# Sample attention of a two-layer decoder step: cached pages turned on VectorE in 32x32 blocks, scores formed in four row groups of TensorE

## The reference, cut to what matters

```
past = cache_latent[l][page_table].reshape(8, 2048, 288)
keys = concat([past, latent])                              # 2048 + 8 rows of 288
q_lat = einsum('bqhn,chn->bqhc', q_nope, w_uk)             # queries taken into the latent
s = einsum('bqhd,bkd->bhqk', concat([q_lat, q_rope]), keys) * SCALE, masked causally
p = softmax(s)
o = einsum('bhqk,bkd->bqhd', p, keys[..., :256])
```

## Time and profile before

| | |
|---|---|
| time, median of 3 runs | 2258.92 us (2255.19 to 2260.28) |
| time of the profiled execution | 2255.74 us |
| its span, first to last instruction | 2254.0 us |
| mean granted TensorE clock | 0.997 |
| busy: TensorE / VectorE / ScalarE / GpSimd | 2210.7 / 1170.6 / 874.9 / 655.1 us |
| transferred | 230.69 MB, mean 102 GB/s |
| chain that ended last | TensorE 96%, VectorE 2%, ScalarE 1% of the span |

### The profile page before, as it was taken

One profiled execution on the slowest core, in us unless ns is written; L12 is line 12 of the kernel. 1 busy time (PEld: TensorE's weight loads), 2 busy tenths in 40 slices (PEclk: granted clock), 3 DMA queues, 4 the chain that ended last, 5 costly groups with the idle time before them and its releaser, 6 DMA issues.

```text
span 2254.0 us, 42639 instructions
## 1 busy us (share of the span) xinstructions
PE 2210.7 (98%) x16239; PEld 1981.8 (88%) x16239; DVE 1170.6 (52%) x1831; ACT 874.9 (39%) x1815; POOL 655.1 (29%) x316
## 2 busy tenths in 40 slices
PE   7999999999999999999999999999999999999998
PEld 5899997667789999999988999966677999999998
DVE  4443753844346666651153717457443476666433
ACT  4223225832234555541132332366322355555322
POOL 0223433400022333333322334342000323333332
PEclk9999999999999999999999999999999999999999
DMA  9554332033333222235545333212332422222332
GB/s 302 170 145 100 85 85 66 19 109 108 85 130 91 79 84 84 84 109 167 173 126 176 83 97 83 79 43 63 97 108 57 156 70 83 79 80 83 87 85 84
DMA packets 338278, 230.69 MB, mean 102 GB/s; under 512 B 62732, under 2 KB 321605, under 8 KB 338140
## 3 DMA queue, kind: packets, MB, share of 16 engines
q1 hardware_dynamic: 336594, 226.37, 35.1%
q10 hardware_dynamic: 1546, 2.43, 0.4%
HBM read 223.15 MB, written 5.60 MB: 101 GB/s over the span
## 4 chain that ended last, share of the span: by engine, by line
PE 96%; DVE 2%; ACT 1%; DMA 0%; issue 0%; DVEq 0%; SPq 0%; ACTq 0%
PE PS L1550 62%; PE PS L1518 7%; PE PS L2000 5%; PE PS L2047 5%; PE PS L1912 3%; PE PS L1833 2%; PE PS L1646 2%; PE PS L1594 2%; PE PS L1936 2%; PE PS L1567 1%; PE PS L1889 1%; PE PS L1994 1%; PE PS L1950 1%; PE PS L2076 0%; DMA rows_in<-x_sample 0%
## 5 line engine op out<-in xcount | busy, mean ns | idle before, releaser
L975 POOL TENSOR_TENSOR wlo<-raw,whi 128x1024 fp32r<-128x1024 f32 (+1 forms) x248 | 586.0, 2363 | 1493.5 <-ACT whi L563 1493.5
L1550 PE MATMUL PS<-h_hi,whi 128*128 128x288 f32 x2496 | 740.7, 297 | 1.2 <-issue 1.0
L1550 PE MATMUL PS<-h_hi,wlo 128*128 128x288 f32 x2496 | 737.1, 295 | 0.0
L1550 PE MATMUL PS<-h_lo,whi 128*128 128x288 f32 x2496 | 737.0, 295 | 0.0
L563 ACT ACTIVATE whi<-raw 128x1024 fp32r<-128x1024 f32 (+1 forms) x252 | 258.4, 1025 | 919.6 <-PE PS L1550 823.5
L1550 PEld LDWEIGHTS PS<-h_hi,whi 128*128 128x128 f32 x2496 | 470.9, 189 | 9.4 <-issue 8.8
L1550 PEld LDWEIGHTS PS<-h_lo,whi 128*128 128x128 f32 x2496 | 471.0, 189 | 0.2
L1550 PEld LDWEIGHTS PS<-h_hi,wlo 128*128 128x128 f32 x2496 | 470.5, 188 | 0.0
L1452 DVE TENSOR_SCALAR conv<-zext,convp 128x592 f32<-128x592 f32 x88 | 153.6, 1746 | 132.5 <-ACTq L894 132.1
L1550 PE MATMUL PS<-act_hi,whi 128*128 128x288 f32 x704 | 209.9, 298 | 0.0
L1550 PE MATMUL PS<-act_hi,wlo 128*128 128x288 f32 x704 | 207.8, 295 | 0.0
(11 more groups left out here) (288 smaller groups left out, 3410.8 us busy)
## 6 DMA issues: line engine op xcount, KB each, us to landing
raw<-w_up SPq DMA_DIRECT2D x88, 512.0 KB, 3.8
pages<-cache_latent SPq DMA_DIRECT2D x256, 144.0 KB, 2.1
raw<-w_in SPq DMA_DIRECT2D x64, 512.0 KB, 4.0
ada_ring<-w_ada SPq DMA_DIRECT2D x41, 512.0 KB, 4.9
raw<-w_down SPq DMA_DIRECT2D x32, 512.0 KB, 3.9
ada_next<-w_ada SPq DMA_DIRECT2D x17, 512.0 KB, 4.0
ada_first<-w_ada SPq DMA_DIRECT2D x16, 512.0 KB, 10.4
raw<-w_out SPq DMA_DIRECT2D x16, 512.0 KB, 4.5
```

The lines of the kernel that those rows point to most:

```text
L975: nc.gpsimd.tensor_tensor(wlo[:, slot, 0:n], raw[:, slot, 0:n], whi[:, slot, 0:n].bitcast(F32), ALU.subtract).then_inc(lo_ready.sem, 1)
L1550: r = mm(PS[0:m, 2 * (j % pairs) + half, 0:HT], w, o[:, k0 + k, half * HT:half * HT + HT], start=(first and k == 0 and part is whi and o i ...
```

## The change

VectorE takes over the turning of the pages. One `transpose` (`turned_keys`) takes 32 columns of all 16 pages, 128 x 512 numbers in a step, and turns each 32x32 block in place of the array: in partition quarter r it leaves the 32 dimensions of the chunk for the 32 positions that quarter r held. Nine such chunks (the rotary one first) make one sequence; they go through a ring of four buffers. TensorE multiplies each chunk in four products with contraction 32, one for each partition quarter r, into bank r. Bank r so holds the positions of quarter r of every page, and the exponential writes `sc` back in page order by its access pattern. `turn_rope`, `turn_keys`, their copies and `rope_scores` are gone.

The queries must now lie in each quarter for every chunk (`qrep`, nine chunks less the rotary one): SP copies them by transfers for b = 0 and 1, ScalarE for the others in 16 small copies (`spread_queries`). The rotary queries are spread by three transfers instead of by VectorE. SP reads the 16 page numbers of a sequence before it waits for the buffer. VectorE takes one maximum over the four banks. ScalarE copies three groups of turned probabilities, VectorE two. On VectorE the first four chunks of b+1 are turned before the gate tile of b, and the others at the head of the next round. On TensorE all nine chunks of sequence 0 now stand ahead of the values of the last pair of heads.

```diff
     pages = [at(f"pages{i}", [128, NPG, LAT], o) for i, o in enumerate((raw_at, arena, cq_at + KD * B))]
-    keysT = [at("keysT0", [128, 2, 512], ckv_at), at("keysT1", [128, 2, 512], arena + 18432)]
-    ropeT = [at("ropeT0", [128, 512], ckv_at + 4096), at("ropeT1", [128, 512], arena + 22528)]
+    NT, RING = LAT // 32, 4
+    keysT = at("keysT", [128, RING, 512], ckv_at)
+    qrep = [at(f"qrep{i}", [128, NT - 1, 128], o) for i, o in enumerate((work + 5120, q_at + 18432, q_at + 22528))]
...
+                numbers = page_numbers(0)
                 sp.wait_ge(unit_used.sem, unit_used.at(l, U_OUT))
-                keys_of(0)
-                sp.wait_ge(qlat_p.sem, qlat_p.at(l, 1))
+                keys_of(0, numbers)
+                sp.wait_ge(qrs_own.sem, qrs_own.at(l, 1))
+                for r in range(1, 4):
+                    sp.dma_start(qrs[32 * r:32 * r + 32].rearrange("p b h s -> p (b h s)"), qrs[0:DR].rearrange("p b h s -> p (b h s)")).then_inc(qrs_in.sem, 16)
+                sp.wait_ge(qlat_ev.sem, qlat_ev.at(l, 1))
+                queries_of(0)
+                sp.wait_ge(k_asm.sem, k_asm.at(l, NH // 2))
+                queries_of(1)
+                numbers = page_numbers(1)
                 sp.wait_ge(k_asm.sem, k_asm.at(l, NH))
...
                 for b in range(3, NB):
+                    numbers = page_numbers(b)
                     sp.wait_ge(spv.sem, spv.at(l, b - 2))
-                    keys_of(b)
+                    keys_of(b, numbers)
...
-                    nc.scalar.activation(sc[:, 0:PAST], PS[:, 0:4, :].rearrange("p a b -> p (a b)"), ACT.Exp,
+                    nc.scalar.activation(sc[:, 0:PAST].rearrange("p (j a i) -> p a j i", j=NPG, a=4), PS[:, 0:4, :].rearrange("p a (j i) -> p a j i", j=NPG), ACT.Exp,
...
+                def spread_queries(b):
...
+                    for r in range(4):
+                        for k in range(4):
+                            last = nc.scalar.activation(qrep[query_slot(b)][32 * r:32 * r + 32].rearrange("p (c k) n -> p c k n", c=KC)[:, :, k, :],
+                                                        qlat[32 * k:32 * k + 32, :, b].rearrange("p c h s -> p c (h s)"), ACT.Copy)
...
                 for b in range(NB):
...
                     exponentials(b)
+                    if b + 2 < NB:
+                        spread_queries(b + 2)
...
+                def turned_keys(b, chunks):
+
+                    for c in chunks:
+                        n, d = NT * b + c, (c - 1) % NT
...
+                        if n >= RING:
+                            dve.wait_ge(multiplied.sem, multiplied.at(l, n - RING + 1))
+                        v.transpose(keysT[:, n % RING, :].rearrange("p (j i) -> p j i", j=NPG), pages[b % 3][:, :, 32 * d:32 * d + 32]).then_inc(turned.sem, 1)
+
                 for h in range(NH):
                     maxima(h)
+                    if h == NH - 1:
+                        turned_keys(0, range(RING))
...
-                    if h == 3:
-                        for j in range(1, 4):
-                            last = v.tensor_copy(qrs[32 * j:32 * j + 32], qrs[0:DR])
-                        last.then_inc(qrs_ready.sem, 1)
...
                 for b in range(NB):
-                    scores(b)
+                    turned_keys(b, range(RING, NT))
+                    new_scores(b)
+                    maximum(b)
+                    if b == 0:
+                        out_pair(NH // 2 - 1)
+                        v.drain()
+                    else:
+                        turned_scores(b - 1)
+                        denominator(b - 1)
+                    if b + 1 < NB:
+                        turned_keys(b + 1, range(RING))
                     v.tensor_tensor(gate_b[:, b, 0:TP], gate_b[:, b, 0:TP], uext[:, b, 0:TP], ALU.add)
                     if b > 0:
-                        outputs(b - 1)
-                outputs(NB - 1)
+                        output(b - 1)
...
+                def scores(b, chunks):
...
+                        pe.wait_ge(turned.sem, turned.at(l, n + 1))
+                        for r in range(4):
+                            rows = slice(32 * r, 32 * r + 32)
+                            q = query(qrs[rows], b) if c == 0 else qrep[slot][rows, c - 1, :]
+                            last = mm(PS[:, r, :], q, keysT[rows, n % RING, :], start=c == 0, stop=c == NT - 1)
+                        last.then_inc(multiplied.sem, 1)
...
                     if h == NH - 1:
-                        pe.wait_ge(expd.sem, expd.at(l, 4 * NH))
-                        turn_rope(0)
+                        scores(0, range(6))
+                        new_scores(0)
+                        scores(0, range(6, NT - 1))
+                        pe.wait_ge(new_ev.sem, new_ev.at(l, 1))
                     turn_probs(h)
-                turn_keys(0, 0)
+                scores(0, range(NT - 1, NT))
                 pair_values(NH // 2 - 1)
...
                 def all_scores(b):
...
+                    scores(b, range(2))
                     if b >= 2:
                         turn_output(b - 2)
...
+                    scores(b, range(2, 6))
                     new_scores(b)
-                    scores(b, 3)
+                    scores(b, range(6, NT))
```

More of the change, by code:

```diff
@@ L291, in build @@
     y_ready, q_roped, gated = signal("y_ready", 4), signal("q_roped", 1), signal("gated", KD, 2)
[L292 removed]
+    qlat_p, qlat_ev, qrs_own = signal("qlat_p", 1), signal("qlat_ev", 1), signal("qrs_own", 1)
+    qrs_in = signal("qrs_in", 3 * 16)
+    qrep_in = [signal(f"qrep_in{i}", 16 * 16) for i in range(2)]
+    qrep_copied = signal("qrep_copied", NB - 2)
     q_asm, k_asm, k_rope = signal("q_asm", NH), signal("k_asm", NH), signal("k_rope", 2)
@@ L332, in ada_at, with query_slot @@
         return range(n, min(n + 2, 5 * KD))
-    def keys_bank(b, g):
-        return 1 if b == 0 and g == 0 else 4
-    def rope_bank(b):
-        return 0 if b == 0 else 6
+    def query_slot(b):
+        return 0 if b == 0 else 1 + (b - 1) % 2
     def last_banks(n):
@@ L474, in _, with page_numbers, keys_of @@
                 wo = A["w_out"]
-                def keys_of(b):
-                    for j in range(NPG):
-                        page = sp.value_load(tab[0:1, b * NPG + j:b * NPG + j + 1], min_val=0, max_val=A["cache_latent"].shape[1] - 1)
+                def page_numbers(b):
+                    return [sp.value_load(tab[0:1, b * NPG + j:b * NPG + j + 1], min_val=0, max_val=A["cache_latent"].shape[1] - 1) for j in range(NPG)]
+                def keys_of(b, numbers):
+                    for j, page in enumerate(numbers):
                         sp.dma_start(pages[b % 3][:, j, :], A["cache_latent"][l, bass.ds(page, 1)].rearrange("b k c -> (b k) c")).then_inc(pages_in[b % 3][j // 4].sem, 16)
@@ L822, in exponentials @@
                     nc.scalar.drain().then_inc(s_exp.sem, 1)
+                def spread_queries(b):
+                    if b == 2:
+                        act.wait_ge(k_asm.sem, k_asm.at(l, NH))
+                    else:
+                        act.wait_ge(multiplied.sem, multiplied.at(l, NT * (b - 1)))
+                    for r in range(4):
+                        for k in range(4):
+                            last = nc.scalar.activation(qrep[query_slot(b)][32 * r:32 * r + 32].rearrange("p (c k) n -> p c k n", c=KC)[:, :, k, :],
+                                                        qlat[32 * k:32 * k + 32, :, b].rearrange("p c h s -> p c (h s)"), ACT.Copy)
+                    last.then_inc(qrep_copied.sem, 1)
                 def turned_scores(b):
-                    for g in (0, 2):
+                    for g in range(3):
                         act.wait_ge(spt_p.sem, spt_p.at(l, 5 * b + g + 1))
@@ L1938, in pair_values @@
                     r.then_inc(pv.sem, 1)
-                def turn_rope(b):
-                    if b >= 2:
-                        pe.wait_ge(spt_a.sem, spt_a.at(l, 2 * (b - 1)))
-                    if b >= 1:
-                        pe.wait_ge(new_ev.sem, new_ev.at(l, b))
-                    for g in range(4):
-                        pe.wait_ge(pages_in[b % 3][g].sem, pages_in[b % 3][g].at(l, 16 * 4 * (b // 3 + 1)))
-                    for t in range(4):
-                        for g in range(4):
-                            r = mm(PS[32 * g:32 * g + 32, rope_bank(b), 128 * t:128 * t + 128], pages[b % 3][:, 4 * g + t, KVL:LAT], ident[:], start=True, stop=True)
-                    r.then_inc(kt_p.sem, 1)
@@ new lines, in scores @@
+                def scores(b, chunks):
+                    slot = query_slot(b)
+                    for c in chunks:
+                        if c == 0:
+                            if b < 2:
+                                pe.wait_ge(qrep_in[slot].sem, qrep_in[slot].at(l, 16 * 16))
+                            else:
+                                pe.wait_ge(qrep_copied.sem, qrep_copied.at(l, b - 1))
+                            if b == 0:
```

(19 more changed lines are left out.)

141 lines of the change are left out of this document (41 added, 100 removed).

## The result

| | before | after |
|---|---|---|
| time, median of 4 runs each on the same chip | 2257.06 us (2255.12 to 2260.28) | 2186.78 us (2184.07 to 2190.99) |
| time and span of the profiled execution | 2255.74, 2254.0 us | 2185.02, 2183.2 us |
| mean granted TensorE clock in it | 0.997 | 0.997 |

The changed kernel takes 0.9689 of the time before, with a 95% interval of 0.9674 to 0.9704: 70.3 us less. The forecast was 2189.5 us. The sum was made against the profiled execution and said 2186.3 for it; it took 2185.02.

What follows compares the result with a forecast made beforehand. TensorE's own work was taken as the bound. Per layer 25.5 (six sequences) plus 7.0 (sequences 0 and 1) plus 2.2 (rotary queries) is 34.7 us; two layers, 69.4 us, off 2258.92 give 2189.5 us, range 2177 to 2218.

Steps and rivals of the forecast that it cites:

- part 1: TensorE without the turning: nine chunks in 8.5 us replace 12.75 us, so a sequence takes 19.2 us, 4.25 less.
- (a): On TensorE, every chunk costs the isolated 1.07 us: 3.1 us gained a sequence, 2205 us in all; chance 0.15.
- part 2: VectorE's nine transposes at 0.75 us each bring it to 12.4 us a sequence, hidden under TensorE's 19.2.
- (b): VectorE becomes the pace: a transpose takes 1.64 us, a sequence 20.9 us, 2215 us in all; chance 0.08.
- (d): VectorE at each round's head: at 2.5 us a transpose a sequence takes 28.6 us, 2341 us in all; chance 0.05.
- turning point: On VectorE, the price of a transpose, 1.98 us, from which (d) makes the kernel slower.
- part 3: ScalarE rises to about 11 us a sequence; exponential and tail end 5.6 us after the scores; hidden, zero cost.
- part 4: SP's pages come about 10 us after their buffer is free, wanted after 13.4 us; zero cost.
- (c): Pages late: SP's full 17.6 us stays behind the wait, a sequence takes at least 20.8 us, 2214 us; chance 0.05.
- part 5: The rotary query copy leaves VectorE after prompt head 3, so the prompt heads gain 2.2 us a layer.
- part 6: Sequences 0 and 1: the scores of sequence 1 end at 480.6 instead of 487.63, 7.0 us earlier.
- clock stretch in the range: TensorE at 1.2 GHz for about 3.4 us behind the wait before sequence 1, worth 1.7 us in each layer.

Runs made afterwards that it cites:

- kernel 10: Changed kernel with the new keys' scores moved beside the turned output, so the nine chunks form two runs, not three; 2184.52 us, ratio 0.9678.
- kernel 11: Changed kernel with the new keys' scores, then the turned output, ahead of all nine chunks in one run; 2181.33 us, ratio 0.9664.
- kernel 12: Order of kernel 11, but the new keys' contraction-32 product stands behind the turned output, directly before the chunks; 2179.57 us, ratio 0.966.
- kernels 2 and 3: Changed kernel with VectorE turning every chunk twice (2214.54 us, ratio 0.9821) and three times (2329.88 us, ratio 1.033).
- kernel 8: Changed kernel with ScalarE's 16 query copies of a sequence made twice; 2201.86 us, ratio 0.9756.
- kernel 1: Changed kernel with each page number read between page transfers again, behind the wait for the buffer; 2199.58 us, ratio 0.9749.
- kernel 4: Changed kernel with VectorE copying the rotary queries after prompt head 3 again, instead of three transfers; 2193.08 us, ratio 0.9722.
- kernel 7: Changed kernel with chunks 1 to 8 in two row groups and 16 identity turns in the pause before sequence 1's scores; 2187.31 us, ratio 0.9692.
- Kernels 5 to 7: Changed kernel with chunks 1 to 8 in two row groups (2205.47 us), in one (2275.92 us), and in two with the pause filled (2187.31 us).

## Why the prediction was right

**TensorE (part 1)** was right in its terms. A round was put at 19.2 us and is 19.21; the nine chunks at 8.5 us and are 8.56. The pace inside a run is 0.872 us against 0.86, the mean surcharge of a run (8.56 - 9 x 0.872) / 3 = 0.24 against 0.27. Rival (a), 1.07 us for each chunk, is out: it needs 9.6 us. The new scores fell from 0.85 to 0.60 us, which was not seen: their last product overlaps a chunk, at some 0.2 us to the run of chunks. The Trainium skill, TensorEngine Tiling (Array Packing), Key Properties, says that changing the tiling mode drains TensorE. The runs agree that a change costs time: one break fewer is worth 0.41 us a round in kernel 10 (0.22 in the chunks, the rest in the full-array products that now stand together), two fewer 0.27 in kernel 11 and 0.37 in kernel 12, where the product with contraction 32 gives some of it back. That the cost is a drain, no row here shows.

**VectorE (part 2)** was right that it is hidden, with a price near the nearest row: 0.70 us (0.75 forecast), and 0.60 from start to start when several follow each other, (2.49 - 0.70) / 3. The maximum over four banks was sized wrongly: 2.29 us, not 2.8. So VectorE needs 11.3 us in a full round, not 12.4. The Trainium skill's figure for VectorE's transpose (VectorE: DVE Perf Modes, The three transpose paths), scaled to 512 columns, gave an estimated 1.24 us; the measured 0.70 decides against that scaling. Rivals (b) and (d) are one mechanism, and it exists. Its turning point was put at 1.98 us from busy time alone; kernels 2 and 3 put it near 1.77, and the end of the cover near 1.3. What failed is the same step in both rivals: busy time leaves out the waits that stand between the parts of VectorE's queue, and (b) spread over the rounds a loss that lies mostly in sequences 0 and 1.

**ScalarE (part 3)**: 16 copies take 6.80 us (6.4 forecast) and the exponential in its new order 1.97, as before. ScalarE's busy time was forecast at 11 us a sequence and is 11.03 in a full round. The exponential and its tail end 501.83 - 495.40 = 6.4 us after the scores (5.6 forecast), within the 9.6 us of values. The maximum is ready at 498.31, but ScalarE starts only at 499.44, when TensorE has turned the last of the old probabilities out of `sc`, a wait that the sum left out. "They delay nobody" held with 6.1 us to spare in a steady round and 2.45 at sequence 1, as kernel 8 shows.

**SP (part 4)**: pages leave in 8.07 us; I had bounded the time behind the wait by the data, about 10 us, with 13.4 allowed. Right, and rival (c) is kernel 1, which was priced at 2214 and costs 2199.6: its rounds average (587.03 - 485.28) / 5 = 20.35 us and not 20.8, since only every second sequence waits, and only sequences 3 to 7 can.

**The rotary queries (part 5)**: 2.2 us a layer, as forecast and as kernel 4 gives back.

**Sequences 0 and 1 (part 6)** gained 8.3 us, not 7.0. Counted from the end of head 14's turn, the scores of sequence 1 were to start 471.2 - 454.14 = 17.1 us later and started 467.25 - 450.98 = 16.3 later. The step that was mis-sized is VectorE's turning of sequence 0: five turns in 3.08 us, so that TensorE hardly waits (0.15 us) where I had it follow VectorE from the fourth chunk on. The other 0.4 us are the scores of sequence 1 themselves, 476.19 - 467.25 = 8.94 us where I had 9.35, because of L1994 and because no turned output cuts the first six chunks of this sequence.

In sum 35.6 us a layer against 34.7. Of the 2.7 us between forecast and median, 1.9 are that the kernel before had a median of 2257.06 in this set and not 2258.92. The clock stretch in the range did not come in the profiled execution (1.00 from 461 to 487 us), but it is real and of the size given: seven of the other kernels with four row groups show it at sequence 1 for some 3.5 us, in one layer or both, at a loss of 1.7. The execution of the changed kernel at a mean of 0.994 took 6 to 7 us longer than those at 0.997.

Left open: why the clock falls behind the same pause in some executions and layers and not in others, and why it fell without a pause in layer 1 of kernel 7. Kernels 5 to 7 show that the pause and the row groups at work both matter, and no more than that.

## What to carry to other kernels

When the chain is TensorE for nearly the whole span, moving layout work to an engine with idle time pays what leaves TensorE's queue less what it must do instead (12.75 us against 8.56 a sequence here), but test the cover by its longest idle piece in the queue's own order and by the first round, which has no neighbour to hide under: busy time overstated both covers here (8.2 us against 6.1 in a steady round and 2.45 at sequence 1 on ScalarE; turning point 1.98 against an estimated 1.77 us on VectorE). Products with contraction 32 in four row groups are nearly free of each other; keep their chunks in one run, put every other product of contraction 32 directly beside that run, and move work that needs nothing ahead of a wait. Read register values for later transfers before the wait on the buffer, not after.

## What the hardware did that I had not expected

- Doing less on TensorE made the program slower. With two of four row groups at work behind a pause of 1.49 us, some 20 us per layer ran at 1.2 GHz and the median rose by 18.7 us; 16 idle turns in the pause took 18.2 of them away. With four groups such a stretch, where it came at all, lasted some 3.5 us. With one group at work the 1.2 GHz level came back in every round with no pause ahead of it (mean clock 0.79 over 120 us), and the time of its one execution was 2275.92 us, above the kernel before.
- Eight instructions with a median of 587 ns, four row groups of two, pass in 0.872 us, the time that one full-array product of the same 512 columns takes (0.86); and a 32-row product of 64 columns starts 0.01 us ahead of a chunk and adds some 0.2 us there (8.14 against 7.94 us for nine chunks), 0.34 us between full-array products.
- A 4-byte 32x32-block transpose of 128 x 512 numbers takes 0.70 us alone and 0.60 in a row, as long as the plain copy from PSUM that it replaced (0.69).
- SP issues a page in 0.50 us when the page's number is already in a register and in 1.06 us when it must fetch it first (8.07 and 17.01 us for 16).
